# Pair sums of the prompt tiles from TensorE (transposed lists times constant matrices) instead of small additions on VectorE

## The reference, cut to what matters

```
s = einsum('thcd,chkd->thck', q, keys)      # per token, head: two lists of 128 scores
sv, si = top_k(s, 16)                       # the 16 best of each list, with indices
cand = sv[:, :, 0, :, None] + sv[:, :, 1, None, :]          # 16 x 16 pair sums
cidx = si[:, :, 0, :, None] * 128 + si[:, :, 1, None, :]    # the expert each pair names
top, sel = top_k(cand, 16)                  # the 16 best pairs
eidx = take_along_axis(cidx, sel)           # 16 experts per token and head
gate = softmax(top)
act = gelu(einsum('td,thkd->thk', x, u_tab[eidx]))
out = einsum('thk,thkd->td', gate * act, v_tab[eidx])
```

## Time and profile before

| | |
|---|---|
| median of the three runs | 1908.96 us |
| the profiled execution, its own time | 1909.85 us |
| its span (first to last instruction on the core) | 1908.0 us |
| mean granted TensorE clock, of full speed | 0.757 |
| instructions | 17956 |
| bytes moved | 687.23 MB, 360 GB/s over the span |

### The profile page before, as it was taken

The page is one execution under the profiler, slowest core; times in us unless marked ns, Lnnn a source line. Parts: engine busy times, 40 slices in busy tenths (PEclk is TensorE's granted clock), DMA queues, the critical chain, the costliest instruction groups (busy, mean ns, idle before and its releaser), DMA issues.

```text
span 1908.0 us, 17956 instructions
## 1 busy us (share of the span) xinstructions
PE 989.2 (52%) x6274; PEld 461.0 (24%) x6274; DVE 1017.8 (53%) x2806; ACT 173.8 (9%) x297; POOL 1126.3 (59%) x1062
## 2 busy tenths in 40 slices
PE   7867411059866462068655776017894520045546
PEld 4434201024422221043111343004341110021113
DVE  1257899932562759755500486883265379960001
ACT  2222110000100110001000022000010000000001
POOL 0033465763567657853577776774456677767770
PEclk9898755579978685588778977557996765567888
DMA  7586787999999999998999999999998999999993
GB/s 295 182 306 265 294 300 290 371 352 415 387 397 401 412 415 344 324 367 313 374 405 409 407 405 408 314 391 361 404 388 331 391 411 409 410 409 409 409 409 123
DMA packets 173191, 687.23 MB, mean 360 GB/s; under 512 B 19856, under 2 KB 21520, under 8 KB 158366
## 3 DMA queue, kind: packets, MB, share of 16 engines
q0 software_dynamic: 152064, 553.72, 75.2%
q1 hardware_dynamic: 21038, 132.37, 17.8%
HBM read 679.88 MB, written 6.59 MB: 360 GB/s over the span
## 4 chain that ended last, share of the span: by engine, by line
DMA 28%; POOL 26%; PE 20%; DVE 13%; issue 11%; ACT 1%; SPq 0%; POOLq 0%; DVEq 0%; ACTq 0%
POOL rows L1196 26%; PE bank L740 9%; DMA rows<-in_v,index_tb 8%; PE acc L1022 7%; DMA rows<-in_v,index_ta 5%; DMA rows<-in_u,index_A 5%; DMA rows<-in_u,index_B 5%; DVE rows L1796 4%; DMA wring<-in_w 3%; DVE scratch L1584 1%; PE bank L737 1%; DMA rows<-in_u,index_S 1%; PE bank L942 1%; DVE scratch L1736 1%; PE bank L987 1%
## 5 line engine op out<-in xcount | busy, mean ns | idle before, releaser
L1196 POOL DMA_INDIRECT rows<-in_u,index_A x256 | 310.4, 1213 | 275.2 <-DVE index_A L1771 183.7
L1022 PE MATMUL acc<-rows,wz 128*32 128x512 f32 x2048 | 325.6, 768 | 205.4 <-DMA rows<-in_v,index_tb 137.5
L740 PE MATMUL bank<-wring,turned 128*128 128x512 f32 x832 | 400.2, 631 | 37.4 <-DMA wring<-in_w 30.8
L1196 POOL DMA_INDIRECT rows<-in_v,index_ta x256 | 245.6, 960 | 199.3 <-PE acc L1022 133.2
L1196 POOL DMA_INDIRECT rows<-in_u,index_B x256 | 294.6, 1151 | 108.8 <-issue 71.6
L1796 DVE SCALAR_TENSOR_TENSOR rows<-rows,xn_b 128x1024 f32<-128x1024 f32 x256 | 308.6, 1225 | 68.5 <-DMA rows<-in_u,index_B 62.6
L1796 DVE SCALAR_TENSOR_TENSOR rows<-rows,xn_a 128x1024 f32<-128x1024 f32 x256 | 306.8, 1225 | 69.1 <-DMA rows<-in_u,index_A 64.5
L1196 POOL DMA_INDIRECT rows<-in_v,index_tb x256 | 240.8, 941 | 142.3 <-issue 66.0
L740 PEld LDWEIGHTS bank<-wring,turned 128*128 128x128 f32 x832 | 161.5, 202 | 235.1 <-issue 198.6
L1022 PEld LDWEIGHTS acc<-rows,wz 128*32 128x32 f32 x2048 | 70.5, 128 | 420.0 <-issue 415.8
L987 PE MATMUL bank<-xn_s,consts 128*128 128x128 f32 x256 | 33.8, 297 | 228.6 <-DVE rows L1791 145.4
(11 more groups left out here) (293 smaller groups left out, 1021.2 us busy)
## 6 DMA issues: line engine op xcount, KB each, us to landing
wring<-in_w SPq DMA_DIRECT2D x108, 1024.0 KB, 8.3
scratch<-in_c_s SPq DMA_DIRECT2D x2, 2064.0 KB, 11.7
out_c_s<-scratch SPq DMA_DIRECT2D x2, 2064.0 KB, 12.8
rows<-in_u,index_A POOLq DMA_INDIRECT x256, 7.9
rows<-in_v,index_ta POOLq DMA_INDIRECT x256, 7.7
rows<-in_u,index_B POOLq DMA_INDIRECT x256, 13.0
rows<-in_v,index_tb POOLq DMA_INDIRECT x256, 7.8
keys<-in_keys SPq DMA_DIRECT2D x2, 1024.0 KB, 9.4
```

What stands on the lines that cost most here:

```text
L740: ins = pe.matmul(ps[:, :], turned["A"][:, 4 * h + c, :], w[:, c, :], start=first, stop=end, skip_group_check=True)
L1022: ins = pe.matmul(acc[i * QUAD:(i + 1) * QUAD, c, :], wz[:, i, g * QUAD:(g + 1) * QUAD], row, start=first, stop=end, skip_group_check=True)
L1196: pool.indirect_dma_start(out=rows[:, n % RING, :], out_offset=None, in_=a[table], in_offset=bass.IndirectOffsetOnAxis(ap=which[:, at:at + ...
```

## The change

`candidates()` lists the 50 pairs in the order of the before-kernel's additions. Two constant matrices of 128 rows and 200 columns, `pick_sum` and `pick_code`, hold for four heads side by side a 1 (and for the codes 128 and 1) at the two list places of each pair. For every prompt call but head 0 of tile 0, a new stage `lists` casts the indices on VectorE, transposes values and indices of up to four heads on TensorE and copies both to SBUF on ScalarE. `pairs` is then two matmuls with the constant matrices on TensorE and one copy by ScalarE into `sums` and `codes`. In layer 1, VectorE adds 128 to the first list's indices in place of the offset in `base`. Head 0 of tile 0 and the sample tiles keep the additions. The table of needs becomes `lists` after `rank`, and `pairs` after `lists` and `sources`; the set of ranking stages gets `lists`.

```diff
-           ("lane_sum", P), ("key0", 64), ("key1", 64), ("own_token", 8), ("head_of", PH), ("place", CANDS), ("eps", 1)]
+           ("lane_sum", P), ("key0", 64), ("key1", 64), ("own_token", 8), ("head_of", PH), ("place", CANDS), ("pick_sum", 4 * CANDS), ("pick_code", 4 * CANDS), ("eps", 1)]
...
+def candidates():
+
+    half, out = TOPK // 2, []
+    for early in (True, False):
+        for r in range(half):
+            lo, hi = (0, half // (r + 1)) if early else (half // (r + 1), STAIR[r])
+            if (hi - lo, lo) not in ((1, 0), (1, 1)):
+                out += [(r, c) for c in range(lo, hi)]
+        for r0, r1, c in ([(half // 2, half, 0)] if early else [(half // 2 + 1, half, 1), (half, TOPK, 0)]):
+            out += [(r, c) for r in range(r0, r1)]
+    return out
...
             if p == 0:
+                if h0:
+                    add("lists", big, h0, h1)
                 add("pairs", big, h0, h1)
                 add("best", big, h0, h1)
...
         if p and j % 2:
+            add("lists", big, 2 * j - 2, 2 * j + 2)
             add("pairs", big, 2 * j - 2, 2 * j + 2)
...
-    "pairs": (("DVE", 2.2),), "best": (("DVE", 5.8),), "soften": (("DVE", 0.4), ("ACT", 0.5)), "choose": (("DVE", 0.8),),
+    "lists": (("DVE", 0.3), ("PE", 0.6), ("ACT", 0.4)), "pairs": (("PE", 0.9), ("ACT", 0.5)), "best": (("DVE", 5.8),), "soften": (("DVE", 0.4), ("ACT", 0.5)), "choose": (("DVE", 0.8),),
...
-RANKING = ("rank", "sources", "pairs", "best", "soften", "choose")
+RANKING = ("rank", "sources", "lists", "pairs", "best", "soften", "choose")
...
@@ TensorE
+            def lists(t, h0, h1):
+                m = 2 * TOPK * (h1 - h0)
+                pe.wait_ge(lists_ready, count(("lists",), ("lists", t, h0, h1)))
+                ps = opened("lists", t, h0)
+                for i, src in enumerate((top, top_f)):
+                    ins = pe.transpose(ps[0:m, i * P:(i + 1) * P], src[:, 2 * h0:2 * h1, :].rearrange("p l k -> p (l k)"), const("ident"))
+                closed(ins, "lists", t, h0)
             def pairs(t, h0, h1):
+                if (t, h0) == (0, 0):
+                    return
                 if KIND[t] != "S":
+                    n = h1 - h0
+                    emptied(pe, "lists", t, h0)
+                    ps = opened("pairs", t, h0)
+                    m, width = 2 * TOPK * n, n * CANDS
+                    for i, name in enumerate(("pick_sum", "pick_code")):
+                        ins = pe.matmul(ps[:, i * width:(i + 1) * width], lists_t[0:m, i, :], const(name, m)[:, 0:width],
+                                        start=True, stop=True)
+                    closed(ins, "pairs", t, h0)
                     return
...
@@ ScalarE
+            def lists(t, h0, h1):
+                m = 2 * TOPK * (h1 - h0)
+                ps = full("lists", t, h0)
+                free(act.activation(lists_t[0:m, :, :], ps[0:m, 0:2 * P].rearrange("p (a n) -> p a n", a=2), ACT.Copy),
+                     "lists", t, h0)
+            def pairs(t, h0, h1):
+                if KIND[t] == "S" or (t, h0) == (0, 0):
+                    return
+                ps = full("pairs", t, h0)
+                two = ps[:, 0:2 * (h1 - h0) * CANDS].rearrange("p (a h c) -> p a h c", a=2, c=CANDS)
+                free(act.activation(paired[:, :, h0:h1, :], two, ACT.Copy), "pairs", t, h0)
...
@@ VectorE
+            def lists(t, h0, h1):
+                mine, n = slice(2 * h0, 2 * h1), 2 * (h1 - h0)
+                if layer_of(t) == 0:
+                    after(dve.tensor_copy(top_f[:, mine, :], top_i[:, mine, :]), lists_ready)
+                    return
+                step(dve.tensor_copy(top_f[:, mine, :], top_i[:, mine, :]))
+                of_first = top_f[:, mine, :].rearrange("p (h c) k -> p h c k", c=2)[:, :, 0, :]
+                after(dve.tensor_scalar(of_first, of_first, float(layer_of(t) * EXPERTS // NKEYS), None, ALU.add), lists_ready)
...
             def find_best(t, h0, h1):
                 m, n, half = LANES[KIND[t]], h1 - h0, TOPK // 2
+                if KIND[t] != "S" and (t, h0) != (0, 0):
+                    emptied(dve, "pairs", t, 4 * (h0 // 4) if t else h0)
...
+    for n, (first, second) in enumerate(candidates()):
+        for g in range(4):
+            c["pick_sum"][[g * LANE + first, g * LANE + TOPK + second], g * CANDS + n] = 1.0
+            c["pick_code"][[g * LANE + first, g * LANE + TOPK + second], g * CANDS + n] = [NKEYS, 1.0]
```

More of the change, by code:

```diff
@@ L271 @@
     "sample_args": ("project", "forget"), "sample_read": ("sample_args",), "sample_write": ("sample_read",), "mix": ("heads", "pool"), "turn2": ("mix",),
-    "query": ("turn2", "norm"), "turn_pq": ("query",), "match": ("turn_pq",), "rank": ("match",), "sources": ("rank",), "pairs": ("rank", "sources"),
+    "query": ("turn2", "norm"), "turn_pq": ("query",), "match": ("turn_pq",), "rank": ("match",), "sources": ("rank",), "lists": ("rank",), "pairs": ("lists", "sources"),
     "best": ("pairs",), "soften": ("best",), "choose": ("soften",), "turn_index": ("choose",), "turn_s": ("choose",), "dots": ("norm",),
@@ L615, in build @@
         base, best, best_f, chosen = (sb(n, P, PH, TOPK) for n in ("base", "best", "best_f", "chosen"))
-        sums, codes = (scratch[:, 3168 + i * 400:3168 + (i + 1) * 400].rearrange("p (h c) -> p h c", c=CANDS)
-                       for i in range(2))
+        paired = scratch[:, 3168:3968].rearrange("p (a h c) -> p a h c", a=2, c=CANDS)
+        sums, codes = paired[:, 0], paired[:, 1]
+        lists_t = sb("lists_t", P, 2, P)
         best_i = sb("best_i", P, PH, TOPK, dt=U32)
@@ L1052, in _ @@
                   "sample_write": sample_write, "heads": heads, "pool_r": pool_r, "pool": pool, "mix": mix,
-                  "turn2": turn2, "query": query, "turn_pq": turn_pq, "match": match_keys, "pairs": pairs, "turn3": turn3, "gate": gate,
+                  "turn2": turn2, "query": query, "turn_pq": turn_pq, "match": match_keys, "lists": lists, "pairs": pairs, "turn3": turn3, "gate": gate,
                   "embed": embed, "turn_index": turn_index, "turn_s": turn_s, "dots": dots_s, "weights": weights,
@@ L1385, in _ @@
                   "norm_heads": norm_heads, "pool_r": pool_r, "turn2": turn2, "query": query, "turn_pq": turn_pq,
-                  "match": match_keys, "soften": soften, "turn3": turn3, "gate": gate,
+                  "match": match_keys, "lists": lists, "pairs": pairs, "soften": soften, "turn3": turn3, "gate": gate,
                   "final": final, "gelu": gelu}
@@ L1697, in pairs @@
                     v0, i0, v1, i1 = (pair_s[:, c:c + 1, :] for c in range(4))
-                else:
[L1699 to L1704, removed]
+                elif (t, h0) == (0, 0):
+                    m, first = P, 0.0
+                    step(dve.tensor_copy(top_f[:, 0:2, :], top_i[:, 0:2, :]))
+                    v0, i0, v1, i1 = (src[:, c:c + 1, :] for c in range(2) for src in (top, top_f))
+                else:
+                    return
                 b0 = base[0:m, h0:h1, :]
@@ L1846, in _ @@
                   "sample_args": sample_args_of, "sample_read": sample_read, "sample_num": sample_num,
-                  "sample_write": sample_write, "norm_heads": norm_heads, "scale_heads": scale_heads, "heads": heads, "pool": pool, "mix": mix, "turn2": turn2, "rank": rank, "pairs": pairs,
+                  "sample_write": sample_write, "norm_heads": norm_heads, "scale_heads": scale_heads, "heads": heads, "pool": pool, "mix": mix, "turn2": turn2, "rank": rank, "lists": lists, "pairs": pairs,
                   "sources": sources, "best": find_best, "soften": soften, "choose": choose, "embed": embed,
```

10 lines of the change are left out of this document (5 added, 5 removed).

## The result

The changed kernel took 1896.09 us (median of 14 runs, 1882.04 to 1903.39), the kernel before 1909.33 (14 runs, 1903.12 to 1919.41): ratio 0.9919, 95% interval 0.9897 to 0.9942. I had forecast 1910.5, with 1899 to 1920. The profiled execution took 1895.08 us, its span 1893.3, against 1909.85 and 1908.0.

The account below looks back on a forecast made before the run. The kernel was taken to wait for gathered rows (DMA) over most of the time. Terms 0.5 - 1.3 + 0 + 1.5 + 0.8 + 0 = +1.5 us gave 1910.5 us against the median, range 1899 to 1920.

Parts of the forecast that it names:

- Start: +0.5: First load: 400 more constant columns, 205 kB at 411 GB/s, delay the start by 0.5 us (0 to 1.0).
- Later passes: 0: Six calls after pass 0: VectorE's saving was waiting anyway and delay is covered, so 0 us (-1 to +4).
- VectorE's busy time: Whole kernel: removed additions, less small added instructions, leave VectorE busy about 24 us less, 9.2 of it in pass 0.
- Order: The planner's merge of ranking stages with other work, worked out as a sequence; no time of its own.
- Gap A: Pass 0, head 1's index wait (31.24 us, to 165.57): index 1.3 us earlier (-2.9 to +1.0).
- B: Pass 0, index wait for heads 2-3 (21.09 us, to 209.89): 0 of its own, moves only with Gap A.
- Gap C: Pass 0, index wait for heads 4-5 (8.65 us, to 261.45): index +3.5, 2.0 returned, net +1.5 us.
- Gap D: Pass 0, index wait for heads 6-7 (14.43 us, to 323.61): net +0.8 us after 2.0 returned (-1.5 to +6).
- Given back: Behind Gap C and Gap D: four fewer backlogged dot products free two GpSimd issues, returning 2.0 us in each.
- Each call pays in full: Rival, pass 0: additions sit on the index chain in all four gaps; -9.2 + 0.5, giving 1900; chance 0.12.
- TensorE's queue becomes the wait: Rival: searches in Gap C and Gap D wait behind TensorE's queued work, +6 each; +11.2 in all, 1920; chance 0.14.
- the rival that the backlog costs GpSimd nothing: Rival: back-to-back dot products don't slow GpSimd, so Gap C and Gap D return nothing; +4.0, 1914.5; chance 0.03.

Follow-up runs that it names:

- second profiles: Profiles of the unchanged kernel before and of the changed kernel, both run again on one chip; ratios 0.9993 and 0.9925 against the kernel before.
- before: The kernel before, unchanged, that the change is compared with; 1909.33 us.
- before_2: The kernel before, unchanged, run once more for a profile beside other kernels; 1909.63 us, 0.9993.
- wide_hbm: The kernel before with constants 3039 columns wide in HBM, only the old 2639 loaded, SBUF as before; 1912.78 us, 1.0012.
- shift192: The kernel before with 48 unused columns (192 bytes) behind its constants, ring of rows on a multiple of 128 only; 1910.33 us, 1.0009.
- order_448: The changed kernel's order and constants, all additions on VectorE, 112 unused columns restoring the ring's old alignment; 1912.59 us, 1.0005 against the kernel before.
- sums_later: The changed kernel at the old alignment, TensorE's sums only in tiles 1, 3 and 4, tile 0 adding on VectorE; 1915.65 us, 1.0024 against the kernel before.
- after_448: The changed kernel with 112 unused columns (448 bytes) behind its constants, ring at the old alignment; 1919.28 us, 1.0047 against the kernel before.
- sums_first: The changed kernel at the old alignment, TensorE's sums only in tile 0, other tiles adding on VectorE; 1911.31 us, 1.0013 against the kernel before.
- the first group: Changed kernel, unused columns, new order with VectorE's additions, TensorE's sums in old order, against the kernel before (2031.3 us); 0.9983, 0.9992, 0.9953, 1.0144.

## Why the prediction was wrong

**The step that failed** is "Start: +0.5", the only term for the 400 new columns, with "Later passes: 0" behind it. I counted the columns as bytes to load and not as an address. All later buffers move by 1600 bytes, and the ring of rows falls onto a multiple of 256. Each gathered row then costs 2.4% less where DMA is the limit (410 against 420 GB/s). The gathers move 553.7 MB; at 410 that is 1350 us, at 420 it is 1318, so 32 us at most. The four kernels shifted by 64 or 320 bytes gained 16.7 to 21.5 us by their medians (17.6 to 23.3 by their ratios), and the unused columns 19.0. The rest of the bytes move where something else limits. The busy DMA row had told me that the gathers bound the kernel. I then asked what the change takes off the engines, and not whether it touches the price of a gather. Nor was that among the rivals.

**The account adds up, within its intervals.** Unused columns: 1891.57 - 1910.53 = -19.0. The change at the old alignment: 1919.28 - 1910.55 = +8.7. Sum -10.3; measured -13.2 and -12.7, inside the intervals of the parts (5 to 6 us to either side).

**The change itself** I had at +1.5 with bounds to the slow side; it is +8.7 (+4.4 to +13.8). The order alone makes +2.0 of it (1912.59 - 1910.55, an interval of -4 to +6); the rest came with the sums on TensorE, whose chain I had priced at 1.7 us in gaps C and D and at nothing behind them. Point by point, from one trace each unless said:

- *VectorE's busy time:* 24.3 us less; forecast "about 24".
- *Order:* the merge exactly as worked out. The planner also moved the search of the lists of heads 6-7 from behind ten groups of dot products to ahead of them, which I had not said.
- *Start:* first gather at 112.76 against 112.91; kernels with and without the wide load scatter from 109.5 to 113.8, so +0.5 can't be told.
- *Gap A:* 27.41 against a forecast of near 30, index 1.3 us earlier, as forecast (0.1 earlier in the second profiles, 164.63 against 164.71). *B:* 23.14 against 21, moving with A only, as forecast.
- *Gap C:* index cast at 266.33 against 261.00, +5.3 where I had +3.5 (ends +1.5 and +6). The structure is the forecast one. TensorE and ScalarE, with the search on VectorE that waits for them (start, us, in brackets the idle time before):

```profile
246.10 0.19 DVE L1744 CAST top_f<-top_i 128x64 f32<-128x64 uint32 x1
246.35 0.42 PE L975 MATMUL bank<-consts,top 128*64 128x128 f32 x1 [36.88 <-DVE top_f L1744]
...
246.78 5.95 PE L758 MATMUL bank<-wring,turned 128*128 128x512 f32 x8
...
252.66 1.08 PE L755 MATMUL bank<-wring,turned_s 128*32 128x128 f32 x32
...
253.67 0.69 PE L987 MATMUL bank<-consts,lists_t 64*128 64x100 f32 x4
...
254.45 0.34 ACT L1398 ACTIVATE scratch<-bank 128x200 f32<-128x200 f32 x1 [6.99 <-PE bank L987]
...
255.90 0.32 DVE L1711 MAX8 best<-scratch 128x8 f32<-128x50 f32 x2
```

  From cast to search 9.8 us, where the additions took 2.3: a half-projection in its slow form (5.95; the earlier trace rows had 6.68 and 3.70) and the samples' 1.08 stand between lists and sums. Dot products filled most of that time: VectorE stood for 2.3 us, as forecast, though what it waited for was rows and not ScalarE's copy.
- *Gap D:* wait 11.47 against 17 forecast; the gather behind it starts at 331.81 against 323.61: +8.2, of which 5.3 are C's. But most of this lateness is the order's and not TensorE's. With the ring at its old place, the waits C and D end so long after the first gather: 147.0 to 148.9 and 208.7 to 213.0 us in the old order (`before`, `before_2`, `wide_hbm`, `shift192`); 153.8 and 220.2, 153.0 and 221.2 in the new order with VectorE's additions in tile 0 (`order_448`, `sums_later`); 156.2 and 220.8, 152.9 and 215.5 with TensorE's sums (`after_448`, `sums_first`). What the new order has in all four is the two more groups of dot products that I had counted ahead of each index; beyond them TensorE's chain adds nothing here that can be told. The two waits of `order_448`, whose first gather starts at 113.52:

```profile
267.34 1.80 POOL L1215 DMA_INDIRECT rows<-in_u,index_A  x1 [13.36 <-DVE index_A L1801]
333.70 0.94 POOL L1215 DMA_INDIRECT rows<-in_u,index_A  x1 [15.48 <-DVE index_A L1801]
```

- *Given back:* more than forecast. From the last index of tile 0's u rows to its first v row it took 50.7 us before (374.27 - 323.61) and 45.5 after (377.29 - 331.81); it is 44.4 in `after_448`, so this is not the cheaper row. Behind D the first six issues of GpSimd followed one another every 1.24 to 1.43 us (331.81 to 339.54) where before they took 2.1 to 2.3 each: VectorE now had other work between its dot products until 337.2. From there they ran back to back, and from 339.54 on the spacing was 2.29. So at that first v row only +3.0 is left of 8.2. In size it is the earlier trace rows once more.
- *Later passes:* forecast 0 (-1 to +4), and here the chain was mis-sized. I priced the chain at 2 to 3 us per call "if TensorE comes at once", and then took what VectorE saves there as waiting anyway. VectorE's waits for a search, and all six of the later calls:

```profile
DVE best L1711 <- ACT scratch L1398: 31.0, 6, 8.8
```
```profile
507.52 0.33 DVE L1711 MAX8 best<-scratch 128x8 f32<-128x50 f32 x2 [2.68 <-ACT scratch L1398]
...
544.91 0.33 DVE L1711 MAX8 best<-scratch 128x8 f32<-128x50 f32 x2 [2.68 <-ACT scratch L1398]
...
891.61 0.33 DVE L1711 MAX8 best<-scratch 128x8 f32<-128x50 f32 x2 [7.74 <-ACT scratch L1398]
...
932.49 0.33 DVE L1711 MAX8 best<-scratch 128x8 f32<-128x50 f32 x2 [8.80 <-ACT scratch L1398]
...
1397.10 0.33 DVE L1711 MAX8 best<-scratch 128x8 f32<-128x50 f32 x2 [5.51 <-ACT scratch L1398]
...
1436.72 0.33 DVE L1711 MAX8 best<-scratch 128x8 f32<-128x50 f32 x2 [3.63 <-ACT scratch L1398]
```

  In these six calls 6 x 2.61 = 15.7 us of additions went, and 31.0 us of standing still came. Tile 1's two cost 2.68 each, as priced. Tile 3's cost 7.74 and 8.80; at the first of them TensorE had a group of v rows ahead of the lists, and that group waited for its rows:

```profile
883.68 0.20 DVE L1748 TENSOR_SCALAR top_f<-top_f 128x64 f32<-128x64 f32 x1
...
884.41 3.64 PE L1059 MATMUL acc<-rows,wz 128*32 128x512 f32 x16 [4.75 <-DMA rows<-in_v,index_tb]
...
887.99 0.48 PE L975 MATMUL bank<-consts,top 128*128 128x128 f32 x1
...
889.21 1.70 PE L987 MATMUL bank<-consts,lists_t 128*128 128x200 f32 x4 [0.53 <-ACT lists_t L1390]
```

  The forecast did name that ("the planner puts vals ahead of it") and gave it no price. `sums_later`, which has these six waits and no others (26.9 us in all), took 6.6 us more than the kernel before by the medians (1915.65 - 1909.05; 4.6 by the ratio), where the same order without TensorE's sums took 2.0 more (1912.59 - 1910.55). That part of the 31 us reaches the end is likely and not shown: the intervals overlap.

**What stays open:** by which waits TensorE's sums lose their time and how the loss splits between pass 0 and the later passes, why the old order costs them 1.4%, and why the first group's gathers ran at 365 GB/s.

**The rivals.** "Each call pays in full" gave 1900, nearest to the median, and is still wrong: with the shift taken away the changed kernel is slower than the one before. "TensorE's queue becomes the wait" came nearest to the change's own cost (+11 forecast, +8.7 measured), but put it in gaps C and D, which are as late without a sum on TensorE, and where most was given back. Against the rival that the backlog costs GpSimd nothing stands the spacing after the change: 2.29 us beside back-to-back dot products (339.54 to 341.83), and 1.24 to 1.43 before that.
The page "SBUF — State Buffer" of the Trainium skill, section "Who interferes with whom", has a VectorE instruction with two SBUF inputs contend with a GpSimd instruction that reads SBUF and not with one that only writes, and it infers that descriptor generation needs the write side. The profile shows the issue reading its index tile (`rows<-in_u,index_A`), so both traces agree with the page's rule. They speak only against the inference, on which my rival rested.

**A better version.** 64 unused bytes in the kernel before give 0.9908 and 0.9878, the change as made 0.9919 and 0.9925. In the one group at full rate that holds both, unused columns alone are 6.3 us below the changed kernel, with intervals that overlap. So the best version of these is the old kernel with its ring aligned; the new order with VectorE's additions, aligned, took 1888.0, which can't be told from it.

## What to carry to other kernels

When a change adds or widens a buffer, work out where every later buffer lands before pricing anything else; test a gain by giving the old kernel the same bytes unused, and the new one the old address. Where gathers bound the kernel, their price per row is the first number to ask about, and a stretch in which no compute engine works is where to read it. Moving small work from a busy engine to an idle one adds a place in that engine's queue: price what stands there, its waits for DMA too, and not the operation alone.

## What the runs showed of the hardware

Gathers of 128 rows of 4096 bytes into SBUF went at 419 to 420 GB/s where the destination began on a multiple of 256 bytes (offsets 0 and 256 past a multiple of 512; 415 and 417 in the v stretch of two traces) and at 409 to 410 where it began 128 or 192 past one (407 in one trace), on full DMA engines. In no trace do two issues of GpSimd follow one another by less than 1.24 us, which is 524,288 / 1.24 = 423 GB/s. In the v stretch shown above 80 of the 89 issues came at that pace after the change, 66 of 86 before. So the aligned rate may be the issue's limit rather than that of the transfers; what aligned transfers could do beyond it no run here shows.
The page "DMA: Bandwidth & Descriptors" of the Trainium skill, section "How a descriptor splits into AXI transactions", says that a descriptor is split into transactions of 256 bytes and that one which reads begins on a 256-byte boundary, so that an unaligned start costs extra beats. Boundary and direction agree with these runs, though here it was the written side that moved. An estimate from its rule: a start 192 past the boundary would fetch 4288 bytes for 4096, 4.7% more, and one 128 past it 4224, 3.1%. The two offsets measured the same 409 to 410 GB/s, 2.4% below the aligned rate. The issue's limit may hide a part of the gain, but not a difference between the two, so the size doesn't follow from that rule.
